# Sparse attention: a batch's four groups transposed in a row, then four scored, then four value groups

## What is computed

```python
top_val, top_idx = lax.top_k(isc, top_k)            # 256 keys of up to 2048 for each query
s = einsum(q_lat, c_sel) * (HEAD_DIM ** -0.5)       # scores against the chosen latents
s = s - slopes * dist                               # ALiBi
s = where(sel_ok, s, -inf)
p = softmax(s)
o_lat = einsum(p, c_sel)
return einsum(o_lat, w_uv)                          # then times a SiLU gate
```

## Time and profile before

| | kernel before |
|---|---|
| median of 3 runs | 3833.8 us |
| profiled execution, its time | 3833.4 us |
| profiled execution, its span | 3831.6 us |
| TensorE (PE) busy | 3536.3 us, 92% |
| VectorE (DVE) busy | 2252.8 us, 59% |
| ScalarE (ACT) busy | 1969.8 us, 51% |
| mean granted TensorE clock | 0.970 |

### The profile page before, as it was taken

One profiled execution on the slowest core, in us unless ns is written; L12 is line 12 of the kernel. 1 busy time (PEld: TensorE's weight loads), 2 busy tenths in 40 slices (PEclk: granted clock), 3 DMA queues, 4 the chain that ended last, 5 costly groups with the idle time before them and its releaser, 6 DMA issues. The chain is left out here.

```text
span 3831.6 us, 85294 instructions
## 1 busy us (share of the span) xinstructions
PE 3536.3 (92%) x33612; PEld 3008.2 (79%) x33612; DVE 2252.8 (59%) x5755; ACT 1969.8 (51%) x4396; POOL 763.1 (20%) x788
## 2 busy tenths in 40 slices
PE   5999999989999989979779999987899999999899
PEld 5777899978777778857658988976777787777787
DVE  6110101057788863320799999968777777777422
ACT  5222211147676652212777667554677777777411
POOL 3222100012567640002005425225100000000000
PEclk9999999989999999989899999988999999999999
DMA  5333321198222123452313364256522122221332
GB/s 187 115 115 115 131 63 62 50 173 225 57 79 79 49 92 111 155 195 104 84 40 126 124 183 138 88 172 212 152 68 66 56 71 79 79 72 44 129 124 81
DMA packets 351732, 416.59 MB, mean 109 GB/s; under 512 B 18921, under 2 KB 256105, under 8 KB 350441
## 3 DMA queue, kind: packets, MB, share of 16 engines
q1 hardware_dynamic: 286584, 318.55, 28.8%
q10 hardware_dynamic: 64768, 92.81, 6.7%
HBM read 247.21 MB, written 164.10 MB: 107 GB/s over the span
## 5 line engine op out<-in xcount | busy, mean ns | idle before, releaser
L1388 PEld LDWEIGHTS s_o<-s_v,s_pT 128*64 128x64 f32 x13056 | 401.1, 138 | 51.8 <-issue 40.1
L230 PE MATMUL s_acc<-s_wh,s_hT 128*128 128x256 f32 (+1 forms) x1408 | 429.9, 305 | 8.0 <-ACT s_parts L653 4.0
L1388 PE MATMUL s_o<-s_v,s_pT 128*64 128x64 f32 x13056 | 434.2, 224 | 0.7 <-issue 0.7
L232 PE MATMUL s_acc<-s_wh,s_hT 128*128 128x256 f32 (+1 forms) x1408 | 429.2, 305 | 0.0
L231 PE MATMUL s_acc<-s_wl,s_hT 128*128 128x256 f32 (+1 forms) x1408 | 429.1, 305 | 0.0
L1545 ACT ACTIVATE s_probs<-s_probs,s_nmx 128x512 f32<-128x512 f32 (+3 forms) x640 | 417.4, 659 | 11.2 <-DVE s_nmx L1591 11.2
L230 PE MATMUL s_acc<-s_hT,s_wh 128*128 128x512 f32 x880 | 349.4, 397 | 55.2 <-DVE s_wl L329 25.7
L1580 DVE CUSTOM_DVE_ANT_0 s_probs<-s_s,s_scores 128x512 f32<-128x512 f32 (+3 forms) x640 | 374.0, 608 | 14.9 <-PEq L91 7.8
L2338 DVE TENSOR_SCALAR_CACHE_REDUCE s_scratch<-s_scores,s_thr 128x384 uint8<-128x384 f32 (+4 forms) x320 | 365.3, 1208 | 1.1
L231 PE MATMUL s_acc<-s_hT,s_wh 128*128 128x512 f32 x880 | 345.8, 393 | 0.0
L232 PE MATMUL s_acc<-s_hT,s_wl 128*128 128x512 f32 x880 | 345.4, 392 | 0.0
(11 more groups left out here) (277 smaller groups left out, 7429.4 us busy)
## 6 DMA issues: line engine op xcount, KB each, us to landing
fm<-s_parts ACTq DMA_DIRECT2D x120, 512.0 KB, 2.8
s_y<-y SPq DMA_DIRECT2D x32, 640.0 KB, 5.6
y<-s_g SPq DMA_DIRECT2D x18, 1024.0 KB, 5.7
kc<-s_parts SPq DMA_DIRECT2D x32, 512.0 KB, 3.2
s_w<-in_o_fm SPq DMA_DIRECT2D x25, 512.0 KB, 4.5
s_w<-in_o_w_in SPq DMA_DIRECT2D x12, 1024.0 KB, 5.5
s_qh<-fm SPq DMA_DIRECT2D x42, 256.0 KB, 3.2
s_ql<-fm SPq DMA_DIRECT2D x42, 256.0 KB, 3.7
```

The source lines that it names most:

```text
L230: nc.tensor.matmul(out, sh, mh, start=(j == 0), stop=False)
L232: ins = nc.tensor.matmul(out, sl, mh, start=False, stop=(j == n - 1))
L1388: last = nc.tensor.matmul(o_ps[r:r + HD, 0:HD], pT[:, x * P + r:x * P + r + HD], v[:, g.u.kbs[g.a + x], vc:vc + HD], start=(g.first and x ...
```

## The change

TensorE's loop of the sparse attention is written in another order. The four transposes of a batch come in a row, then its two calls of `score` (four groups), then four value groups. Before, the two calls of `score` stood between the second and the third transposed group. No instruction is added or taken away, no wait is, and the orders of the other engines, the buffers and the transfers stay.

```diff
                 for n in range(0, NG, BATCH):
-                    turn(n)
-                    turn(n + 1)
+                    for x in range(n, n + BATCH):
+                        turn(x)
                     if n + LEAD < NG:
                         score(n + LEAD)
                         score(n + LEAD + 2)
-                    turn(n + 2)
-                    turn(n + 3)
                     if n:
                         for x in range(n - BATCH, n):
                             feed(x)
```

## The result

| | before | changed |
|---|---|---|
| median | 3830.45 us (4 runs, 3825.37 to 3835.72) | 4051.51 us (4 runs, 4046.49 to 4055.81) |
| profiled span | 3831.6 us | 4044.7 us |
| mean granted clock | 0.970 | 0.955 |

The ratio is 1.0576, with a 95% interval of 1.0555 to 1.0597: 221 us slower. The forecast was 4019 us with a range of 3965 to 4075.

What follows compares the result with a forecast made beforehand. TensorE was taken to bound the stage: 8.6 + 17.5 - 5.4 = 20.7 us a pair of heads, +161 us over the stage, plus 25 us for the clock on 3833.4 us gave 4019 us, range 3965 to 4075.

Steps and rivals of the forecast that it cites:

- What bounds the stage: In the transposes' stage, some 834 us of the span, TensorE sets the pace and whatever it waits longer counts.
- Cost 1: Second pair of transposes waits for ScalarE's copy of group n: 0.43 us a batch, 8.6 us a pair of heads.
- Cost 2: Group n+3's transposes wait for VectorE's copy of n+1, late behind its biases and outputs: 17.5 us a pair of heads.
- heavy batch: Batch with four or eight VectorE outputs before its copy, three per pair of heads: TensorE stands still 3.0 us with four.
- What goes away: TensorE's waits on score banks vanish, 5.4 us a pair of heads; step from scores to values taken as 0.19 us.
- The clock: TensorE's granted clock falls after most heavy waits in the stage, adding 25 us.
- The signs: Profile marks: transposes wait some 130 us for VectorE's copy, singly near 3 us; a pair of heads takes 124 to 128 us.
- (1): Rival: VectorE keeps up in the stage, only the wait for ScalarE's copy is left; 3857 or 3900 us, 8%.
- (2): Rival: VectorE's copies are late in the stage but the clock stays up; 3995 us, 22%.
- (3): Rival: faster, as a batch loses one 0.148 us step and 43 us of bank waits vanish; 3767 us, 3%.
- (4): Rival: no change, the extra waits are hidden since VectorE has the pace in the stage anyway; 3%.
- Rival 5: Clock falls for longer, whole batches run at the lower level and slow transposes delay the next copy; 4080 to 4150 us, 9%.

Runs made afterwards that it cites:

- outputs_early: The changed kernel with VectorE's outputs of a batch moved from between its biases to directly behind its copy: 3903.89 us, 1.0190 of before.
- three_and_one: The changed kernel with three transposed groups in a row, then the scores, the fourth group and the values: 3908.25 us, 1.0203 of before.
- filler: The changed kernel with extra transposes ahead of the real ones in five batches per pair of heads where TensorE waits long for VectorE: 3989.24 us, 1.0421 of before.

## Why the prediction was right

- **What bounds the stage.** Right: TensorE's waits counted in full. The other stages did not move. The first transpose of the stage starts at 2742.3 us before and at 2740.2 after, and from the start of the last one to the end of the span it is 265.4 and 265.8 us.
- **Cost 1**, 0.43 us a batch, 67 us: right in mechanism, a little small. Two kernels that differ in TensorE's order alone lie 74 us apart, 0.47 us a batch. The prediction took the second pair's start from its load of weights (1.45 us) and the scores' start from the product. From product to product give 1.48 us, and 84 of the 85 full pairs in the changed kernel's profile show 1.47 or 1.48 us. Less 1.02 that is 0.46 us.
- **Cost 2**, 17.5 us a pair: right in mechanism. The heavy batch came out at 7.23 us where 7.18 was worked out. outputs_early and three_and_one each take it away from one side and land within 5 us of each other. Its size is known as a remainder only: 124.5 us for a pair without the clock, less the 98.7 without waits and the 9.5 of cost 1, leaves some 16.3 us.
- **What goes away**, 5.4 us a pair: right. One wait on a score bank is left in the profile after, and a pair without waits takes 98.7 us where 98.4 was counted on. The step from scores to values is as long as the one from scores to transposes, as was taken.
- **The sum without the clock**: +161 us, 124.5 us a pair. filler, where the clock stays up, measured +161 us and 124.4 to 124.7 us. That it is so close is partly luck: cost 1 was taken 0.9 us a pair too small, and cost 2 some 1.2 us too large.
- **The clock** is the term that was mis-sized: 25 us predicted, 55 to 62 us measured. I expected one fall after most of the 22 heavy waits and counted none after the shorter ones, and let part of the slow time lie under VectorE's time. All 22 heavy waits brought a fall, in seven pairs the first one a stretch twice as long as the others, and ten falls came behind shorter waits. The 1.5 us that one stretch was said to cost was about right, but with the long ones counted twice there were 39 of them, 58 us. And VectorE hides little. The slow stretch lies over scores and values, and the next copy then waits for TensorE, not TensorE for it: VectorE stands idle for 1.73 us before its copy at 2872.55 (the rows of VectorE above). Of the 133 us at half the clock at most half, 66 us, could be lost, and 55 to 62 were. My bound of 66 us was for two stretches after each of the 22, so the measured value lies near its end. This is why the time came out near the upper end of the 3985 to 4060 us given to the forecast.
- **The signs.** Waits on VectorE's copy sum to 110 us in the profile (some 130 were named), with 22 single waits near 3 us. A pair was to take 124 to 128 us. It took 133 us where five falls came and 130.3 where three did, which is the clock again.
- **The rivals** fell: VectorE did not keep up (1), the clock did not stay up (2), the kernel was neither faster (3) nor unchanged (4). Rival 5 was close in kind, since the clock fell more than forecast, but not in size.

## What to carry to other kernels

A copy can be late at no cost as long as its consumer has other work first. Before moving that work, read from the timeline when the copy really ends, not when it could. When two buffers alternate, a write into one of them starts at the earliest when the write before it into the same one has been copied out (here 1.48 us from start to start, with four tiles in each bank). Fill that time with the write into the other buffer and with other work; scores or values did alike here. Where TensorE must wait a microsecond or more now and then, count the slower clock behind the waits as well. And spread small bookkeeping of the copying engine to where it idles: on the kernel before, this and moving one copy of four to ScalarE brought 1.1%.

## What was not expected of the hardware

In the stage before, 21 waits of TensorE of 1.21 to 1.44 us brought one fall of the granted clock. In the changed kernel nine of 16 waits of 1.14 to 1.57 us did, and all 22 of 2.8 to 3.1 us. A wait of 1.34 us was followed by a fall at one place and not at another; the cause of that is open. Filling 1.0 to 2.2 us of the waits of 1.5 us and more (by the layout of the prediction) with useless transposes kept the clock at 1.00 and brought the whole kernel from 4051.51 to 3989.24 us: extra work in a wait can pay for itself.
